# A hybrid decoder layer on one core: the head groups of the delta rule written out, their output moved to another buffer, and steps moved between pieces

## The chip, the cores and the metric

The kernel runs on one core of one Trainium2 chip. The metric is device time in microseconds (us), from the start of the program to its end. Three runs of the kernel before took 2874.61, 2876.35 and 2878.93 us; the median is 2876.35.

## What is computed

One layer of a decoder for a prompt of 256 tokens and 8 sample tokens (264 columns in all), with a model width of 2048. The part that matters here is the mixer's input projection and its branch A, the gated delta rule with 16 query/key heads and 32 value heads of width 128:

```python
proj = rmsnorm(h, attn_norm) @ w_in
q, k, v, z, a, b, sB, sC, sh, gA, gB = jnp.split(proj, IN_SPLITS, axis=-1)
qkv, new_qkv = causal_dwconv(jnp.concatenate([q, k, v], axis=-1), s_qkv, qkv_conv_w)
q, k, v = jnp.split(jax.nn.silu(qkv).astype(jnp.float32), (KEY_DIM, 2 * KEY_DIM), axis=-1)
q, k = l2norm(q), l2norm(k)                     # per head, each repeated for two value heads
...
decay = jnp.exp(jnp.where(lower, G[..., :, None] - G[..., None, :], -jnp.inf))
kk = jnp.einsum('bhncd,bhnsd->bhncs', k, k)
A = jnp.where(strict, beta[..., :, None] * kk * decay, 0.0)
sol = lax.linalg.triangular_solve(eye + A, rhs, left_side=True, lower=True)
...
o = rmsnorm(o, gdn_norm) * jax.nn.silu(z)       # gated output of each head
y_a = o.reshape(Bn, T, VAL_DIM) @ w_gdn_out
```

After the mixer come the merge with branch B, the output projection, a SwiGLU FFN, a per-layer input embedding and a final norm.

## The kernel before

Everything is written by hand per engine; the order within an engine is the order of the code, and the engines meet at semaphores. The weights stream from HBM in pieces of 4 row tiles x 256 columns (512 KB). For each piece SyncE starts the load into `raw` (4 buffers), ScalarE copies a rounded half `whi` (line 941, called here a split), VectorE subtracts to get the rest `wlo` (L1233), and TensorE does 24 matmuls over 264 columns (3 products for each of 8 blocks, L668). ScalarE and VectorE work three pieces ahead of TensorE. Four pieces make a pair of output tiles, which VectorE and ScalarE then scale, convolve and store (`evac`).

The columns of `w_in` for the delta rule are walked in 8 head groups, each of 4 value heads. A group is 32 pieces, numbered 0 to 31: k, q, v0, v1, z0, sc, sh and z1, four pieces each. The first group is a phase of its own ("first", with one more pair of four pieces ahead of it, so that its piece 0 is the phase's piece 4); the other seven are the phase "groups", a hardware loop of seven rounds; after it six pairs of sb columns ("last_group") carry the rest of the last group.

Between the pieces stand the steps of the delta rule. Three tables, `PE_STEP`, `ACT_STEP` and `DVE_STEP`, say after which piece of TensorE, and after which piece's split on ScalarE and VectorE, a step is placed; "cur" is the group whose columns are being made, "prev" the one before, whose last steps run during pieces 0 to 6 of the next. The steps spoken of here are:

- `exponents` (VectorE, L1285): differences of the cumulated decays, from `blk` into `E`; `exps` (ScalarE, L979, L980): their exponentials, into `EG` and `E`.
- `kk` (TensorE, L697 and the four matmuls behind it): transposes and products of the keys; it needs the SiLU of k (ScalarE, L1081, whose code stands after the split of piece 5), `exponents`, and `olog` of the group before, which frees its PSUM banks. `kcopy` (ScalarE, L984, L987) and `lt` (VectorE, L1314) make the lower triangle `Tt` from it.
- `blk_store` (ScalarE, L991): four DMAs write the 32x32 diagonal blocks of `Tt` to `blk_scratch`. GpSimd reads them back into `blk` (`blocks_in`, L556), solves them (`solve`, L535 to L542), writes `sol_scratch` (L564) and reads it into `DT` (L568). `blk` also holds the decay rows for `exponents`; they are loaded for the next group behind the solve (L548).
- `pt` (TensorE, after piece 25): the first products with `DT`. It waits for `DT` to land. `t1` stands after piece 31.
- `o1` (TensorE, after piece 3 of the next group), `osq`, `osum`, `oroot` and `o`: the output of the group, its norm, and its product with the gate in `o_all` (VectorE, L1361, L1366). The output stands in `E`, so that `exponents` of the next group waits for `o`.
- `qsum` after piece 11, with ones times the squares of q; `qn` on VectorE after the split at piece 13; `qk` on TensorE after piece 14.

GpSimd's queue of a group is, in order: two state loads of the group (`st_qkv`, L516, each waiting until TensorE has turned the state two loads before), `st_sc`, `finish` of the group before (stores, and a wait until they have landed), two state loads of the next group, `blocks_in`, `solve`, `solution_out`, the decay rows, `tails_out`. The first state load of the next group waits for TensorE's turn at piece 8, the second for the one at piece 12.

The functions that the diff touches, with the profile's line numbers:

Of the kernel before, what the change touches and what calls it, by code (L numbers as in the profile page):

```python
# [44 lines left out]
SB = 32  # L45
# [45 lines left out]
def trunk(nc, I, O):  # L91
# [133 lines left out]
    with ctx:  # L225
# [22 lines left out]
        ea_ready, diag_ready, tok_turned = (sem(n) for n in ("ea_ready", "diag_ready", "tok_turned"))  # L248
# [66 lines left out]
        nxt, cur = (lambda it: it + 1), (lambda it: it)  # L315
        const = lambda n: (lambda it: n)
        def layer_pairs(gx):
# [4 lines left out]
            Phase("groups", NG - 1, layer_pairs(nxt)),  # L322
# [54 lines left out]
        def cur_of(ph, it):  # L377

            return 0 if ph.name == "first" else it + 1 if ph.name == "groups" else None

        def prev_of(ph, it):

            return it if ph.name == "groups" else NG - 1 if ph.name == "last_group" else None

        def steps(table, ph, it, j):
# [3 lines left out]
            for which, gr in (("prev", prev_of(ph, it)), ("cur", cur_of(ph, it))):  # L389
                if gr is not None:  # L390
                    out += [(s, gr) for s in table[which].get(b, ())]
# [18 lines left out]
        PE_STEP = {"cur": {7: ("kk",), 11: ("qsum", "nturn"), 14: ("qk",), 18: ("tails",), 19: ("vturn",),  # L410
                           25: ("pt",), 26: ("pt0",), 27: ("pe0",), 28: ("pf0",), 29: ("s1",), 30: ("ks",), 31: ("t1",)},
                   "prev": {0: ("pt1",), 1: ("pe1",), 2: ("pf1",), 3: ("o1",), 4: ("osum",), 5: ("sct",)}}
        ACT_STEP = {"cur": {7: ("exps",), 8: ("kcopy",), 9: ("blk_store",), 10: ("qsq",), 12: ("qroot", "ncopy"),
                            19: ("stage",), 20: ("vcopy",), 25: ("t0c",), 27: ("f0c",), 29: ("s1c",), 31: ("t1c",)},
                    "prev": {1: ("f1c",), 3: ("osq",), 4: ("oroot",), 6: ("sct",)}}
        DVE_STEP = {"cur": {6: ("exponents",), 7: ("lt",), 13: ("qn",), 15: ("qkt",), 25: ("mask",), 26: ("e0",),
                            27: ("ktok",), 28: ("u0",), 30: ("r",)},
                    "prev": {0: ("e1",), 2: ("u1",), 3: ("s2",), 6: ("o",)}}
# [54 lines left out]
        def _(pool):  # L473
            mine = Count(pool_self)
            SOLVE_OPS = 2 * SB - 1
# [36 lines left out]
            def load_state(grp, i):  # L512
                if not (i < 2 and isinstance(grp, int) and grp == 0):
# [64 lines left out]
            def group(grp, first, last):  # L578
# [84 lines left out]
        def _(pe):  # L663
# [15 lines left out]
            def gdn(slot, gr):  # L679
# [990 lines left out]
```

## Time and profile before

| | |
|---|---|
| median of three runs | 2876.35 us |
| the profiled execution | 2873.98 us, its span 2872.4 us |
| TensorE matmul busy | 2694.1 us, 94% of the span |
| VectorE busy | 1658.9 us, 58% |
| ScalarE busy | 1344.4 us, 47% |
| GpSimd busy | 429.7 us, 15% |
| mean granted TensorE clock | 0.957 of full |
| HBM traffic | 175 GB/s over the span |

The rows below come from one profiled execution. PE is TensorE, DVE VectorE, ACT ScalarE, POOL GpSimd. A row of the timeline is start, duration, engine, line, operation, output<-inputs, tile sizes and count; in square brackets is the idle time of the engine before it and what ended that. A PE row's duration is that of pipelined matmuls, so the distance between starts tells more than the duration. The clock is given as a share of full speed (2.4 GHz); 0.5 is 1.2 GHz.

### The profile page before, as it was taken

The numbers are of one execution on the slowest core, as the hardware profiler recorded it, in microseconds if no ns is written. First come the engines' busy times: TensorE is split into PE (matmuls) and PEld (weight loads), VectorE is DVE, ScalarE is ACT, GpSimd is POOL, SyncE is SP. The second block draws the span as 40 slices with busy tenths as digits, with TensorE's granted clock in tenths as the row PEclk, the third lists the DMA queues.
The fourth block names the chain that finished last, engine by engine and source line by source line (L and its number), as shares of the span: only waits on it lengthen the run. The fifth ranks groups of instructions, "written<-read, shape, count | busy, mean of one in ns | idle before, by whom it ended". The sixth has DMA issues, their size and how long they took to land.

```text
span 2872.4 us, 57080 instructions
## 1 busy us (share of the span) xinstructions
PE 2694.1 (94%) x21133; PEld 2651.4 (92%) x21133; DVE 1658.9 (58%) x2851; ACT 1344.4 (47%) x2024; POOL 429.7 (15%) x813
## 2 busy tenths in 40 slices
PE   6989898888888989999999999899999999999997
PEld 4989898888888889999999999899999999999987
DVE  4747474747474656553335555555666656776664
ACT  4535353534344445443334434344555545665553
POOL 1324151515151505000000000000011000100000
PEclk9999999999999999999999999999999999999999
DMA  5545353535353535666665555755898566986552
GB/s 168 166 119 156 113 157 109 161 104 159 103 159 110 154 109 155 173 188 191 183 195 158 174 179 168 232 170 160 261 312 289 181 197 206 318 286 194 164 164 91
DMA packets 449338, 505.31 MB, mean 176 GB/s; under 512 B 27713, under 2 KB 429882, under 8 KB 446338
## 3 DMA queue, kind: packets, MB, share of 16 engines
q1 hardware_dynamic: 415264, 415.42, 48.1%
q0 software_dynamic: 24640, 86.42, 9.3%
q8 instruction: 120, 1.97, 0.3%
q10 hardware_dynamic: 9282, 1.24, 0.3%
q14 instruction: 32, 0.26, 0.0%
HBM read 477.10 MB, written 26.49 MB: 175 GB/s over the span
## 4 chain that ended last, share of the span: by engine, by line
PE 76%; POOL 8%; DMA 4%; issue 4%; DVE 3%; ACT 3%; POOLq 0%; ACTq 0%; DVEq 0%; SPq 0%
PE bank L668 75%; POOL prod L539 4%; POOL sol L542 4%; ACT whi L941 1%; DMA blk<-blk_scratch 1%; DMA raw<-in_w_ffn_down 1%; DMA raw<-in_w_o 1%; DMA sol_scratch<-sol 1%; DMA DT<-sol_scratch 1%; DVE wlo L1233 0%; ACT xhi L955 0%; DVE E L1285 0%; POOLq L73 0%; POOL sol_scratch L564 0%; POOL DT L568 0%
## 5 line engine op out<-in xcount | busy, mean ns | idle before, releaser
L668 PE MATMUL bank<-xhi,whi 128*128 128x264 f32 x5520 | 1618.9, 293 | 34.4 <-DVE wlo L1233 17.0
L668 PE MATMUL bank<-xlo,whi 128*128 128x264 f32 x5520 | 1593.3, 289 | 0.0
L668 PE MATMUL bank<-xhi,wlo 128*128 128x264 f32 x5520 | 1590.3, 288 | 0.0
L1233 DVE TENSOR_TENSOR wlo<-raw,whi 128x1024 fp32r<-128x1024 f32 x828 | 1012.1, 1230 | 817.6 <-ACT whi L941 815.4
L941 ACT ACTIVATE whi<-raw 128x1024 fp32r<-128x1024 f32 x828 | 872.3, 1058 | 926.3 <-PE bank L668 850.1
L668 PEld LDWEIGHTS bank<-xhi,whi 128*128 128x128 f32 x5520 | 1067.4, 193 | 40.9 <-issue 32.1
L668 PEld LDWEIGHTS bank<-xlo,whi 128*128 128x128 f32 x5520 | 1067.9, 193 | 2.6 <-issue 1.9
L668 PEld LDWEIGHTS bank<-xhi,wlo 128*128 128x128 f32 x5520 | 1064.4, 193 | 0.0
L668 PE MATMUL bank<-ahi,whi 128*128 128x264 f32 x704 | 200.6, 285 | 3.7 <-DVE wlo L1233 3.7
L668 PE MATMUL bank<-ahi,wlo 128*128 128x264 f32 x704 | 200.6, 285 | 0.0
L668 PE MATMUL bank<-alo,whi 128*128 128x264 f32 x704 | 200.2, 284 | 0.0
L668 PEld LDWEIGHTS bank<-ahi,whi 128*128 128x128 f32 x704 | 133.0, 189 | 3.9 <-DVE wlo L1233 3.9
L668 PEld LDWEIGHTS bank<-ahi,wlo 128*128 128x128 f32 x704 | 133.1, 189 | 0.0
L668 PEld LDWEIGHTS bank<-alo,whi 128*128 128x128 f32 x704 | 132.9, 189 | 0.0
L539 POOL TENSOR_TENSOR prod<-blk,sol 128x60 f32<-128x60 f32 (+24 forms) x248 | 117.3, 473 | 19.5
L542 POOL TENSOR_TENSOR sol<-sol,prod 128x60 f32<-128x60 f32 (+24 forms) x248 | 115.3, 465 | 19.4
L1378 DVE SCALAR_TENSOR_TENSOR cacc<-cin,vec,cacc 128x288 f32<-128x288 f32 x224 | 107.5, 521 | 14.8 <-DVE cacc L1376 2.3
L641 POOL DMA_DIRECT2D out_gdn_s<-sS x16 | 18.7, 1168 | 608.9 <-DVE sS L1597 608.9
L516 POOL DMA_DIRECT2D st_qkv<-in_state_qkv_conv x32 | 16.6, 520 | 532.0 <-PE bank L668 532.0
L1152 ACT ACTIVATE sS<-sS,bc 128x128 f32<-128x128 f32 x256 | 81.2, 392 | 0.0
L1597 DVE SCALAR_TENSOR_TENSOR sS<-sD,kqs,sS 128x128 f32<-128x128 f32 x256 | 72.6, 346 | 0.0
L668 PE MATMUL bank<-DT,Nn 128*128 128x128 f32 x128 | 28.0, 408 | 47.0 <-DMA DT<-sol_scratch 47.0
(279 smaller groups left out, 1902.5 us busy)
## 6 DMA issues: line engine op xcount, KB each, us to landing
raw<-in_w_in SPq DMA_DIRECT2D x356, 512.0 KB, 3.9
raw<-in_w_ffn_gate SPq DMA_DIRECT2D x88, 512.0 KB, 5.0
raw<-in_w_ffn_up SPq DMA_DIRECT2D x88, 512.0 KB, 4.7
raw<-in_w_ffn_down SPq DMA_DIRECT2D x96, 384.0 KB, 3.3
raw<-in_w_gdn_out SPq DMA_DIRECT2D x64, 512.0 KB, 3.6
chunkS<-in_state_gdn POOLq DMA_DIRECT2D x16, 1024.0 KB, 7.6
raw<-in_w_sconv_out SPq DMA_DIRECT2D x32, 512.0 KB, 3.6
raw<-in_w_o SPq DMA_DIRECT2D x32, 512.0 KB, 4.5
```

Of the source, the lines that this page charges most:

```text
L516: pool.dma_start(st_qkv[:, i % 2, :, :], stq[:, ds(STATE_COL[i](grp), COLS)].rearrange("r (t p) -> r t p", p=P)).then_inc(st_in[i % 2], 16)
L539: mine.inc(pool.tensor_tensor(prod[:, 0:m, 0:n], blk[:, j, j + 1:SB].unsqueeze(1).to_broadcast([P, m, n]), sol[:, 0:m, j:j + 1].to_broadca ...
L542: mine.inc(pool.tensor_tensor(sol[:, 0:m, j + 1:SB], sol[:, 0:m, j + 1:SB], prod[:, 0:m, 0:n], ALU.add))
L641: pool.dma_start(O["gdn_s"][0, 2 * b2 + s, 16 * c:16 * c + 16, :, :].rearrange("h k v -> k h v"), sS[:, s, :, :]).then_inc(n_stored[s], 16)
L668: return pe.matmul(out, lhsT, rhs, start=start, stop=stop)
L941: act.activation(whi[:, at_ % SPLIT, :, :], raw[:, at_ % RAW, :, :], ACT.Copy).then_inc(hi_ready, 1)
L1152: m = act.activation(sS[:, s, i, :], sS[:, s, i, :], ACT.Copy, scale=bc[:, ds(it * 2 + (s + 1), 1), 16 * c + i:16 * c + i + 1].rearrange(" ...
L1233: dve.tensor_tensor(wlo[:, at_ % SPLIT, :, :], raw[:, at_ % RAW, :, :], f32(whi[:, at_ % SPLIT, :, :]), ALU.subtract).then_inc(lo_ready, 1)
L1378: m = dve.scalar_tensor_tensor(out=cacc[:, t, :], in0=x, scalar=w, in1=cacc[:, t, :], op0=ALU.mult, op1=ALU.add)
L1597: m = dve.scalar_tensor_tensor(out=sS[:, s, i, :], in0=sD[:, s, i, :], scalar=kqs[:, 8 * c + i // 2, ds(it * 2 + s, 1), 0], in1=sS[:, s, i ...
```

## The change

The loop over seven groups becomes seven phases of straight code, on all engines; tests for "not the first group" that asked whether the group number was a register now ask for its value. The output of a group is copied into `vTok` instead of `E`, so `exponents` waits for `u1` of the group before instead of `o`, and `vcopy` (piece 20) waits for `o`. `exponents` moves from piece 6 to 3, `exps` from 7 to 4, `kk` and `lt` from 7 to 6, `kcopy` from 8 to 6, `nturn` from 11 to 10, `o` from 6 to 9. `kk` no longer waits for `exponents`. In the first group `exponents` and `exps` stand at 8 and 9 and `lt` at 9. The blocks are stored by GpSimd itself, and it loads the next group's first two states behind the solve instead of ahead of it.

```diff
-            Phase("groups", NG - 1, layer_pairs(nxt)),
+            *[Phase(f"group{n}", 1, layer_pairs(const(n))) for n in range(1, NG)],
...
-        PE_STEP = {"cur": {7: ("kk",), 11: ("qsum", "nturn"), 14: ("qk",), ...
+        PE_STEP = {"cur": {6: ("kk",), 10: ("nturn",), 11: ("qsum",), 14: ("qk",), ...
+                    "first": {9: ("exps",)}}
+                    "first": {8: ("exponents",), 9: ("lt",)}}
...
             def blocks_in(grp):
 
+                pool.wait_ge(g["lt"], grp + 1)
+                pool.sem_inc(pool_passed, 1)
+                for b in range(4):
+                    pool.dma_start(blk_d[:, b, :, :].rearrange("m j i -> j m i"),
+                                   Tt[SB * b:SB * b + SB, :, :].rearrange("p c (i t) -> p (c i) t", i=4)[:, :, SB * b:SB * b + SB]
+                                   ).then_inc(g["blk_stored"], 16)
                 pool.wait_ge(g["blk_stored"], grp * 64 + 64)
...
                 if not first:
                     finish(grp - 1)
-                if not last:
-                    load_state(grp + 1, 0)
-                    load_state(grp + 1, 1)
                 blocks_in(grp)
                 solve(grp)
                 solution_out(grp)
                 if not last:
                     decay_rows(grp + 1)
+                    load_state(grp + 1, 0)
+                    load_state(grp + 1, 1)
                 tails_out(grp)
...
-            with pool.Fori(0, NG - 2) as it_:
-                mine.enter(it_, SOLVE_OPS)
-                group(it_ + 1, False, False)
-            mine.leave(NG - 2)
+            for grp in range(1, NG - 1):
+                group(grp, False, False)
...
                 if slot == "kk":
                     pe.wait_ge(silu_done, 4 * gr + 1)
-                    pe.wait_ge(g["expo"], gr + 1)
-                    if not isinstance(gr, int):
+                    if gr > 0:
                         pe.wait_ge(g["olog"], gr)
+                    else:
+                        pe.wait_ge(tok_ready, 1)
...
-                elif slot == "blk_store":
-                    act.wait_ge(g["lt"], gr + 1)
-                    for b in range(4):
-                        act.dma_start(blk_d[:, b, :, :].rearrange("m j i -> j m i"), ...
...
                 elif slot == "vcopy":
                     act.wait_ge(g["vturned"], gr + 1)
                     act.wait_ge(g["klen"], gr + 1)
+                    act.wait_ge(g["o"], gr + 1)
...
-                    act.activation(E[:, 0, :], bank[6][:, :], ACT.Copy)
+                    act.activation(vTok[:, 0, :, :].rearrange("p b c -> p (b c)"), bank[6][:, :], ACT.Copy)
...
-                    act.activation(E[:, 1, :], bank[7][:, :], ACT.Copy)
+                    act.activation(vTok[:, 1, :, :].rearrange("p b c -> p (b c)"), bank[7][:, :], ACT.Copy)
...
                 if slot == "exponents":
                     dve.wait_ge(g["gb"], gr * 16 + 16)
-                    dve.wait_ge(g["o"], gr + 1)
+                    dve.wait_ge(g["u1"], gr) if gr > 0 else None
...
                 elif slot == "o":
                     dve.wait_ge(g["oroot"], gr + 1)
-                    mine.inc(dve.scalar_tensor_tensor(out=E[:, :, :], in0=E[:, :, :], scalar=vec[:, 368:369], ...
+                    ov = vTok[:, :, :, :].rearrange("p a b c -> p a (b c)")
+                    mine.inc(dve.scalar_tensor_tensor(out=ov, in0=ov, scalar=vec[:, 368:369], in1=PT[:, :, :], op0=ALU.mult, op1=ALU.mult))
                     mine.settle(dve)
                     for c in range(NCH):
                         o = o_all[:, ds(gr * 4, 4), c * CH:(c + 1) * CH]
-                        m = dve.tensor_tensor(o, o, H4(E, c), ALU.mult)
+                        m = dve.tensor_tensor(o, o, vTok[:, c, :, :], ALU.mult)
```

ScalarE, before, in a round of the loop, from the split at piece 6 to `kcopy` (`scb` is the staging of branch B's tail, `EG` and `E` are `exps`):

```order
L941 ACTIVATE whi<-raw 128x1024
L1036 REGISTER_ALU
L1038 ACTIVATE scb<-bank 10x256
L940 REGISTER_ALU
L941 ACTIVATE whi<-raw 128x1024
L979 ACT_TABLE_LOAD
L979 ACTIVATE EG<-blk 128x512
L980 ACTIVATE E<-E 128x1024
L940 REGISTER_ALU
L941 ACTIVATE whi<-raw 128x1024
L984 ACTIVATE Tt,ksum<-bank 128x128 x4
```

And in the changed kernel, a later group, from `oroot`'s exponential (`PT`) through the SiLU of k (`sqk`, `smp`) to `kcopy`:

```order
L1037 ACTIVATE PT<-PT 128x1024
L987 ACTIVATE EG<-blk 128x512
L988 ACTIVATE E<-E 128x1024
L949 ACTIVATE whi<-raw 128x1024
L1084 ACT_TABLE_LOAD
L1084 ACTIVATE sqk<-cacc 128x256
L1085 ACTIVATE smp<-cacc 128x8
L1084 ACTIVATE sqk<-cacc 128x256
L1085 ACTIVATE smp<-cacc 128x8
L949 ACTIVATE whi<-raw 128x1024
L1041 ACTIVATE scb<-bank 10x256
L992 ACTIVATE Tt,ksum<-bank 128x128 x4
```

`exps` now stands directly behind `oroot`, ahead of the SiLU of k; one table load and one split fewer stand between the SiLU and `kcopy`.

GpSimd, before, in a round of the loop, from the last store of `finish` to the solve (`sol<-unit` is its first operation):

```order
L526 DMA out_sc_s<-scb 8x256
L527 ISA
L528 ISA
L514 ISA
L516 ISA
L516 DMA st_qkv<-in_state_qkv_conv 24x256
L516 REGISTER_ALU
L516 DMA st_qkv<-in_state_qkv_conv 24x256
L553 ISA
L556 DMA blk<-blk_scratch 32x1024 x4
L535 COPY sol<-unit 128x256
```

And in the changed kernel:

```order
L530 DMA out_sc_s<-scb 8x256
L560 DMA blk_scratch<-Tt 32x8x32 x4
L566 DMA blk<-blk_scratch 32x1024 x4
L539 COPY sol<-unit 128x256
```

The two state loads, which waited for TensorE, have left this place; the four stores of the blocks have come to it.

VectorE in the changed kernel, a later group, from `s2` (`S`) through `exponents` to the end of the convolution of k (`cin`, `cacc`):

```order
L1359 SCALAR_TENSOR_TENSOR S<-S,bc,bank 128x128 x4
L1288 SCALAR_TENSOR_TENSOR E<-blk,tok,later 128x128 x8
L1442 TENSOR_TENSOR cin<-bank,rstd 128x256
L1443 TENSOR_TENSOR cin<-bank,rstd 128x8
L1444 TENSOR_TENSOR tail<-bank,rstd 128x11
L1445 COPY cin<-bank 128x8x3
L1442 TENSOR_TENSOR cin<-bank,rstd 128x256
L1443 TENSOR_TENSOR cin<-bank,rstd 128x8
L1444 TENSOR_TENSOR tail<-bank,rstd 128x11
L1445 COPY cin<-bank 128x8x3
L1379 TENSOR_SCALAR cacc<-cin,vec 128x288 x2
L1381 SCALAR_TENSOR_TENSOR cacc<-cin,vec,cacc 128x288 x6
```

Before, `exponents` stood behind `o`, behind the convolution and three splits. Now only the splits of pieces 7 to 9 stand between the convolution and `lt`, and `o` follows the convolution of q.

## Rows read from the trace of the kernel before

**Rows 1.** Waits of TensorE, 0 to 1150 us: total us, times, longest.
```profile
PE bank L668 <- DMA DT<-sol_scratch: 47.0, 7, 8.4
PE bank L697 <- DVE E L1285: 36.8, 8, 5.2
PE bank L668 <- issue: 18.3, 6, 3.2
```

**Rows 2.** Timeline of TensorE: `kk` of three groups, and piece 6 of one.
```profile
225.27 1.11 PE L697 MATMUL bank<-ident,sqk 128*128 128x128 f32 x4 [5.15 <-DVE E L1285]
...
497.12 0.37 PE L668 MATMUL bank<-xhi,whi 128*128 128x264 f32 x1
...
508.32 1.11 PE L697 MATMUL bank<-ident,sqk 128*128 128x128 f32 x4 [5.14 <-DVE E L1285]
...
1077.45 1.11 PE L697 MATMUL bank<-ident,sqk 128*128 128x128 f32 x4 [5.15 <-DVE E L1285]
```

**Rows 3.** Timeline of TensorE: marks in the first group and behind the last.
```profile
89.42 0.63 PE L697 MATMUL bank<-ident,sqk 128*128 128x128 f32 x4 [0.81 <-DVE E L1285]
...
101.88 0.36 PE L668 MATMUL bank<-xhi,whi 128*128 128x264 f32 x1 [1.47 <-DVE wlo L1233]
104.87 1.02 PE L668 MATMUL bank<-QK,ones 128*128 128x512 f32 x2
...
186.99 1.05 PE L668 MATMUL bank<-vTok,DT 128*128 128x128 f32 x8
187.97 0.62 PE L668 MATMUL bank<-ident,st_qkv 24*128 24x24 f32 x4
...
202.95 0.38 PE L668 MATMUL bank<-EG,S 128*128 128x128 f32 x2
...
1094.42 1.02 PE L668 MATMUL bank<-QK,ones 128*128 128x512 f32 x2
...
1141.24 1.95 PE L668 MATMUL bank<-DT,Nn 128*128 128x128 f32 x16
...
1166.77 1.05 PE L668 MATMUL bank<-vTok,DT 128*128 128x128 f32 x8
```

**Rows 4.** Timeline of ScalarE: `oroot`, the split behind k's SiLU, `exps`, the next split.
```profile
496.83 1.06 ACT L1034 ACTIVATE PT<-PT 128x1024 f32<-128x1024 f32 x1
...
501.00 1.04 ACT L941 ACTIVATE whi<-raw 128x1024 fp32r<-128x1024 f32 x1
...
508.30 0.63 ACT L979 ACTIVATE EG<-blk 128x512 f32<-128x512 f32 x1 [3.74 <-DVE E L1285]
...
509.79 1.04 ACT L941 ACTIVATE whi<-raw 128x1024 fp32r<-128x1024 f32 x1
```

**Rows 5.** Timeline of VectorE: `o` and `exponents` of one group.
```profile
503.22 1.28 DVE L1361 SCALAR_TENSOR_TENSOR E<-E,vec,PT 128x1024 f32<-128x1024 f32 x1
...
506.08 2.19 DVE L1285 SCALAR_TENSOR_TENSOR E<-blk,tok,later 128x128 f32<-128x128 f32 x8
```

**Rows 6.** Stretches behind two short waits: length, busy (count) per engine, granted clock, DMA.
```profile
1631.90:1636.00 4.10, 4.05 (x33) 4.05 (x34) 4.10 (x13) 2.49 (x5) 0.00 (x0) 1.00 0.03 8
1851.70:1856.00 4.30, 4.25 (x22) 4.25 (x23) 0.00 (x0) 0.00 (x0) 0.00 (x0) 0.60 1.03 376
```

**Rows 7.** Timeline of GpSimd: last state load ahead of `blocks_in`; the last group's blocks.
```profile
528.15 0.51 POOL L516 DMA_DIRECT2D st_qkv<-in_state_qkv_conv  x1 [15.17 <-PE bank L668]
...
1089.53 1.97 POOL L556 DMA_DIRECT2D blk<-blk_scratch  x4 [16.46 <-DMA blk_scratch<-Tt]
1094.41 0.40 POOL L535 COPY sol<-unit 128x256 f32<-128x256 f32 x1 [2.91 <-DMA blk<-blk_scratch]
...
1134.92 2.32 POOL L568 DMA_DIRECT2D DT<-sol_scratch  x4 [3.18 <-DMA sol_scratch<-sol]
```

**Rows 8.** DMA issues by line: count, KB of each, median us to landing.
```profile
blk_scratch<-Tt ACTq DMA_DIRECT2D x32, 32.0 KB, 1.7
sol_scratch<-sol POOLq DMA_DIRECT2D x32, 32.0 KB, 2.6
```

More of the change, by code:

```diff
@@ L247, in trunk @@
             sem(n) for n in ("soft_in", "soft_ready", "g_ready", "rows_ready"))
-        ea_ready, diag_ready, tok_turned = (sem(n) for n in ("ea_ready", "diag_ready", "tok_turned"))
+        ea_ready, diag_ready, tok_turned, tok_ready = (sem(n) for n in ("ea_ready", "diag_ready", "tok_turned", "tok_ready"))
         z_scaled = sem("z_scaled")
@@ L313, in spair @@
             return mk(win, lambda it: b + gx(it) * COLS, X, kind, gx, xr="attn")
-        nxt, cur = (lambda it: it + 1), (lambda it: it)
+        cur = (lambda it: it)
         const = lambda n: (lambda it: n)
@@ L377, in cur_of @@
         def cur_of(ph, it):
-            return 0 if ph.name == "first" else it + 1 if ph.name == "groups" else None
+            return 0 if ph.name == "first" else int(ph.name[5:]) if ph.name.startswith("group") else None
         def prev_of(ph, it):
-            return it if ph.name == "groups" else NG - 1 if ph.name == "last_group" else None
+            return int(ph.name[5:]) - 1 if ph.name.startswith("group") else NG - 1 if ph.name == "last_group" else None
         def steps(table, ph, it, j):
@@ L390, in steps @@
                 if gr is not None:
-                    out += [(s, gr) for s in table[which].get(b, ())]
+                    at_b = table[which].get(b, ())
+                    if ph.name == "first" and "first" in table:
+                        at_b = table["first"].get(b, tuple(s for s in at_b if not any(s in v for v in table["first"].values())))
+                    out += [(s, gr) for s in at_b]
             return out
@@ L407, in freed_all @@
                 eng.wait_ge(pair_free[m % 2], m // 2 + 1)
-        PE_STEP = {"cur": {7: ("kk",), 11: ("qsum", "nturn"), 14: ("qk",), 18: ("tails",), 19: ("vturn",),
+        PE_STEP = {"cur": {6: ("kk",), 10: ("nturn",), 11: ("qsum",), 14: ("qk",), 18: ("tails",), 19: ("vturn",),
                            25: ("pt",), 26: ("pt0",), 27: ("pe0",), 28: ("pf0",), 29: ("s1",), 30: ("ks",), 31: ("t1",)},
                    "prev": {0: ("pt1",), 1: ("pe1",), 2: ("pf1",), 3: ("o1",), 4: ("osum",), 5: ("sct",)}}
-        ACT_STEP = {"cur": {7: ("exps",), 8: ("kcopy",), 9: ("blk_store",), 10: ("qsq",), 12: ("qroot", "ncopy"),
+        ACT_STEP = {"cur": {4: ("exps",), 6: ("kcopy",), 10: ("qsq",), 11: ("ncopy",), 12: ("qroot",),
                             19: ("stage",), 20: ("vcopy",), 25: ("t0c",), 27: ("f0c",), 29: ("s1c",), 31: ("t1c",)},
-                    "prev": {1: ("f1c",), 3: ("osq",), 4: ("oroot",), 6: ("sct",)}}
-        DVE_STEP = {"cur": {6: ("exponents",), 7: ("lt",), 13: ("qn",), 15: ("qkt",), 25: ("mask",), 26: ("e0",),
+                    "prev": {1: ("f1c",), 3: ("osq",), 4: ("oroot",), 6: ("sct",)},
+                    "first": {9: ("exps",)}}
+        DVE_STEP = {"cur": {3: ("exponents",), 6: ("lt",), 13: ("qn",), 15: ("qkt",), 25: ("mask",), 26: ("e0",),
                             27: ("ktok",), 28: ("u0",), 30: ("r",)},
-                    "prev": {0: ("e1",), 2: ("u1",), 3: ("s2",), 6: ("o",)}}
+                    "prev": {0: ("e1",), 2: ("u1",), 3: ("s2",), 9: ("o",)},
+                    "first": {8: ("exponents",), 9: ("lt",)}}
         NORM = {"first": 0, "ffn0r": 1, "pgate_first": 2}
@@ L512, in load_state @@
             def load_state(grp, i):
-                if not (i < 2 and isinstance(grp, int) and grp == 0):
+                if i >= 2 or grp > 0:
                     pool.wait_ge(st_turned, grp * 4 + (i - 1))
@@ L703, in gdn @@
                     pe.wait_ge(g["qsq"], gr + 1)
-                    if not isinstance(gr, int):
+                    if gr > 0:
                         pe.wait_ge(g["s2"], gr)
@@ L708, in gdn @@
                     pe.wait_ge(g["qn"], gr + 1)
-                    if not isinstance(gr, int):
+                    if gr > 0:
                         pe.wait_ge(sct_staged, gr)
@@ L999, in gdn @@
                     act.wait_ge(tails_turned, gr + 1)
-                    if not isinstance(gr, int):
+                    if gr > 0:
                         act.wait_ge(tails_stored, 96 * gr)
@@ L1226, in _ @@
             dve.sem_inc(g["o"], 1)
-            dve_per = {"groups": 20, "gates": 0, "yb1": 0, "ya0": 2, "ya1": 2, "wo": 0,
+            dve_per = {"gates": 0, "yb1": 0, "ya0": 2, "ya1": 2, "wo": 0,
                        "ffn0s": 2, "ffn1s": 2, "down0": 0, "down1": 0, "pgate": 2}
@@ L1551, in extra @@
                     mine.settle(dve)
+                    dve.sem_inc(tok_ready, 1)
                 elif ph.name in NORM and j == 3:
```

6 lines of the change are left out of this document (removed).

## The prediction

> **What bounds the kernel now.** I read the page's busy shares first: TensorE has work in 94% of the span, so a gain can only come from its idle time or its clock. The waits of TensorE up to 1150 us, the stretch of the head groups, come next. Three kinds recur once a group: for `DT`, 47.0 us in 7 waits; for `exponents` ahead of `kk`, 36.8 us in 8, nearly all of it in seven of about 5.15; and 18.3 us in 6 put down to "issue" [rows 1]. These six stand at the turns of the loop, ahead of the first state turn of a round. The loop is seven rounds, so it turns six times.
>
> Next I took the length of a group from `kk` to `kk`. From the second group (225.27) to the last (1077.45) it is 852.18 / 6 = 142.03 us [rows 2]. What TensorE would need without a wait at full clock I put together from stretches where it had none [rows 3]: `kk` to `qsum` 104.87 - 89.42 - 1.47 = 13.98; `qsum` to `pt` 1141.24 - 1094.42 = 46.82; `pt` to `t1` 1166.77 - 1141.24 = 25.53; `t1` to the turn of the next group 187.97 - 186.99 = 0.98; turn to `o1` 202.95 - 187.97 = 14.98; `o1` to the point where `kk` could begin 225.27 - 5.15 - 202.95 = 17.17 [rows 2, 3]. The sum is 119.5. So 22.5 us of each group are not work. The waits are (47.0 - 8.4) / 6 = 6.4 (the first group's 8.4 left out) + 5.15 + 18.3 / 6 = 3.05, together 14.6 [rows 1, 2]. The other 7.9 us I put down to matmuls at half clock behind the three waits.
>
> **The turn of the loop.** Straight code leaves no branch. Between the first group and the loop, where the code is straight too, TensorE went from `t1` to the turn in 0.98 us without a wait [rows 3]. I take the 3.05 us and the slow clock behind them as gone. If only the branch goes and something else waits there, nothing is gained; that is a rival below. Register instructions in the other engines' queues go as well; I cost them at nothing, since these engines are ahead of TensorE except where named below.
>
> **`exponents` and `kk`.** In one group pieces 6 and 7 take 508.32 - 5.14 - 497.12 = 6.06, so 3.0 us each, and piece 6 ended at about 500.15 [rows 2]. `kk` now stands there. `exponents` (2.19 us) moves ahead of the convolution of k on VectorE and is no longer waited for [rows 5]; the convolution gets 2.2 us later and stays ahead of ScalarE. What is late next is the SiLU of k. Before, it was done when the next split began, at 501.00 [rows 4]. Now `exps` stands ahead of it, directly behind `oroot`: 509.79 - 508.30 = 1.49 us, without a table load of its own, because `oroot` ends in the same function [rows 4]. So k is ready at 501.00 + 1.49 = 502.5, and `kk` waits 2.3 us with a handover. Bounds: 0.8 if `exps` costs this path nothing, 4.5 if the late convolution costs it another 2.2. I take 2.3. The piece that leaves the stretch before `kk` comes behind it: no gain and no loss.
>
> **The blocks.** Before, GpSimd reached `blocks_in` only after the state load that waits for TensorE's turn at piece 12 (a wait of 15.17), at 528.15 [rows 7]. In the last group, which has no such loads, it waited for the blocks alone, and TensorE took up `pt` with no wait [rows 3, 7]. That group is the model for all. There, from `kk`: blocks landed after 1089.53 - 1077.45 = 12.1; solve begun after 17.0; the four loads of `DT` issued from 57.5 to 59.8, landed, with the 2.6 of a like GpSimd transfer, at about 62.4 [rows 2, 7, 8]. GpSimd stores the blocks itself now. Four transfers of this size take it as long to issue as the loads of `DT`, 2.3 us, where ScalarE needs a little less, and land in 2.6 instead of 1.7 [rows 7, 8]: up to 1.4 later. But `kk` at full clock ends 1.3 sooner. TensorE reaches `pt` at 13.98 + 3.0 (piece 7) + 46.82 = 63.8 us after `kk`. So `DT` lands 1 to 3 us ahead, and the 6.4 us go with their slow clock. The cover is thin: a solve longer by 3 us uses it up.
>
> **`o` at piece 9.** It took 506.08 - 503.22 = 2.86 us of VectorE [rows 5]. It leaves the path ahead of `kk` and goes between `lt` and `qn`, while `lt` no longer has the split of piece 10 ahead of it. TensorE is nearer to VectorE there than before. I add 1.3 us of wait for `qn`; bounds 0 and 2.9, the whole of `o`.
>
> **Clock.** Behind a wait of 2.56 us the granted clock was 1.00, behind one of 1.91 us 0.60 [rows 6]; so the rows leave open whether 2.3 us costs speed. The three stops of a group cost 7.9 / 3 = 2.6 each. Where the clock falls the wait for `qn` shrinks, since TensorE arrives later. I take 0.8 us a group for both together, bounds 0 and 2.6. The Trainium skill, TensorE: Matmul & The Clock Gate, section Part 1, says that the throttled clock is the default state and that activity releases it; the two rows show that a short wait can go either way. Were each wait to cost the full step, the group would be 1.8 us longer than I take it.
>
> **The sum.** A group: 119.5 + 2.3 + 1.3 + 0.8 = 123.9, against 142.0: 18.1 less, times six, 109. The first group hardly gains: its `lt` moves behind the convolution of q and gets later by about the 7 us that `blocks_in` no longer waits, so `DT` lands near where it did, and its 8.4 us wait stays [rows 1]; bounds minus 5 and plus 5. Its successor's `kk` gains 5.15 - 2.3 = 2.9, and its move by one piece is 3.0, which comes back behind the last `kk`. The last group has no `DT` wait to lose; behind its `kk` it gains about 1.8 of clock and pays 1.3 at `qn`. That makes 109 + 3 = 112. The profiled execution took 2873.98, so it would take 2762. The median before was 2876.35, 2.4 more; I forecast 2763 for the median.
>
> **Rivals.**
> 1. `DT` stays last. For it: the cover is 1 to 3 us, and the solve now lies beside the convolutions of v0 and v1 and `qkt`. Against it: it took no wait in the last group. If it lands 2 us late and the clock falls behind it, a group costs 2.0 + 2.6 = 4.6 more: 7 x 4.6 = 32, hence 2795. Chance 0.17.
> 2. The turn's cost stays, because it was no branch but something else that happens at a group's start. The six "issue" waits speak for it, the smooth start of the second group against it. 6 x (3.05 + 2.6) = 34, hence 2797. Chance 0.07.
> 3. The written-out code itself stops the engines: seven groups of instructions that are fetched once each, where a loop had one. Place: the instruction supply of TensorE; price: that of a turn, 3.05 + 2.6 = 5.65 us a stop. It decides from 112 / 5.65 = 20 stops, three a group. With four a group, 28 x 5.65 = 158, the kernel takes 2763 + 158 = 2921. Against it: up to 1150 us, with the whole first group in straight code, the six turns are the only "issue" waits of TensorE [rows 1]. Chance 0.05. The Trainium skill, Runtime: NRT & Kernel Launch, section Instruction fetch mechanics, says that the sequencer fetches ahead in order and hides it, and that a taken branch breaks this; by that the stops vanish and this rival with them.
>
> **Numbers.** My forecast has 0.71. Its own range is 2745 (no clock loss, no wait at `qn`: 6 x 2.1 less, and the first group plus 5) to 2787 (`kk` waiting 4.5 and the clock falling behind it, 4.0 a group more). The range reaches to rivals 1 and 2: 2740 to 2800. A measurement of this kernel can tell 0.2%, about 6 us, from no change. Faster: 0.71 + 0.17 + 0.07 = 0.95, less 0.01 for mishaps that eat exactly the gain; same 0.01; slower 0.05.
>
> **What the profile after would show.** Right: no "issue" wait of TensorE in the groups; `kk` waiting about 2.3 us for the SiLU of k on ScalarE, not for VectorE's `E`; waits for `DT` gone but for the first group's 8 us; `kk` to `kk` near 124 us; GpSimd's wait for TensorE ahead of the blocks gone. Wrong: a `DT` wait in each group (rival 1), waits at the first state turn (rival 2), "issue" waits strewn over pieces (rival 3), or a wait of TensorE for `wlo` or `sqk` from VectorE above 3 us a group, which would mean that I underrated VectorE's queue between `lt` and `qn`.

## The result and the profile after

The kernel after takes 2788.78 us (median of four runs, 2780.30 to 2792.23); the kernel before took 2875.54 beside it. The ratio is 0.9692, with a 95% interval of 0.9669 to 0.9715: 3.1% faster. The profiled execution took 2788.91 us, its span 2787.2, with a mean clock of 0.971 of full (0.957 before). The forecast was 2763. The time lies in the stated range (2740 to 2800), but only because that range reached out to rivals 1 and 2; the forecast's own ended at 2787. The likeliest case was not the one that happened: the waits for `DT` stayed, which was rival 1 (2795, chance 0.17).

TensorE's waits in the head groups, the view of [rows 1], total, times and longest:

```profile
PE bank L675 <- DMA DT<-sol_scratch: 30.0, 8, 5.6
PE bank L705 <- ACT smp L1085: 16.4, 7, 2.3
PE bank L675 <- DVE wlo L1236: 9.9, 2, 6.3
PE bank L728 <- DVE Tt L1317: 4.2, 1, 4.2
```

The "issue" waits are gone. `kk` waits for the SiLU of k (L1085), 2.35 us in each of seven groups, where it waited 5.15 for VectorE before. The third row is not new: before, the wait for `wlo` was 12.6 us in 4, the longest 6.3 as here. But `DT` is still waited for in all eight groups; four of the waits, and `kk` of the second, the sixth and the last group, from the timeline (start, duration, line, operation, idle time before):

```profile
160.16 3.75 PE L675 MATMUL bank<-DT,Nn 128*128 128x128 f32 x16 [4.87 <-DMA DT<-sol_scratch]
221.23 1.12 PE L705 MATMUL bank<-ident,sqk 128*128 128x128 f32 x4 [2.35 <-ACT smp L1085]
415.01 2.02 PE L675 MATMUL bank<-DT,Nn 128*128 128x128 f32 x16 [0.74 <-DMA DT<-sol_scratch]
730.92 0.66 PE L705 MATMUL bank<-ident,sqk 128*128 128x128 f32 x4 [2.35 <-ACT smp L1085]
797.95 3.56 PE L675 MATMUL bank<-DT,Nn 128*128 128x128 f32 x16 [3.58 <-DMA DT<-sol_scratch]
926.64 3.75 PE L675 MATMUL bank<-DT,Nn 128*128 128x128 f32 x16 [5.57 <-DMA DT<-sol_scratch]
986.83 0.66 PE L705 MATMUL bank<-ident,sqk 128*128 128x128 f32 x4 [2.35 <-ACT smp L1085]
```

A group is (986.83 - 221.23) / 6 = 127.6 us, against 142.0 before and 123.9 forecast. Over groups 2 to 7 the wait for `DT` is 3.6 us on average (0.74 to 5.57). GpSimd's part of the group whose `kk` is at 730.92, to be set beside [rows 7]:

```profile
737.73 2.39 POOL L560 DMA_DIRECT2D blk_scratch<-Tt  x4 [4.03 <-issue]
743.09 2.00 POOL L566 DMA_DIRECT2D blk<-blk_scratch  x4 [2.97 <-DMA blk_scratch<-Tt]
750.00 0.40 POOL L539 COPY sol<-unit 128x256 f32<-128x256 f32 x1 [4.92 <-DMA blk<-blk_scratch]
785.83 2.35 POOL L574 DMA_DIRECT2D sol_scratch<-sol  x4 [0.74 <-POOLq L548]
792.04 2.32 POOL L578 DMA_DIRECT2D DT<-sol_scratch  x4 [3.87 <-DMA sol_scratch<-sol]
```

The solve (750.00 to 785.83, 35.8 us) is nearly as long as before (over the seven later groups 36.1 us on average, from `sol<-unit` to the store of the solution, against 35.4). The transfers are not: GpSimd waits 4.92 us for the blocks where it waited 2.91 in the last group before [rows 7], and 3.87 for the solution. The solve begins 19.1 us after `kk`, not 17.0. The windows of this stretch (us; busy time and count of PE, PEld, DVE, ACT, POOL; clock; DMA share; GB/s) and SyncE's weight loads, issued 6.9, 12.9 and 17.7 us after `kk`:

```profile
742.92:744.92 2.00, 2.00 (x20) 2.00 (x19) 2.00 (x3) 2.00 (x6) 1.83 (x4) 1.00 0.26 68
744.92:746.92 2.00, 2.00 (x20) 2.00 (x19) 1.97 (x3) 2.00 (x4) 0.17 (x1) 1.00 0.85 224
746.92:748.92 2.00, 2.00 (x16) 1.77 (x15) 2.00 (x3) 0.13 (x2) 0.00 (x0) 1.00 1.09 290
748.92:750.92 2.00, 2.00 (x13) 1.44 (x12) 1.96 (x10) 1.98 (x2) 0.76 (x3) 1.00 1.08 300
```

```profile
737.78 0.37 SPq L447 DMA_DIRECT2D raw<-in_w_in  x1
743.79 1.50 SPq L447 DMA_DIRECT2D raw<-in_w_in  x2
748.58 1.50 SPq L447 DMA_DIRECT2D raw<-in_w_in  x2
```

The DMA engines are full (share 0.85 to 1.09) from two us after the first block load is issued until the blocks have landed: the 4 x 128 KB of the blocks run beside two or more weight loads of 512 KB. The weight loads go out when VectorE's `wlo` frees a buffer, and after the convolution of q VectorE does two or more `wlo` in a row, so they come in bunches. Here the two `wlo` ahead of the loads at 743.79 and 744.92, and, of the last group before, the four weight loads that started 1.6 us after its block load [rows 7]:

```profile
742.54 2.35 DVE L1236 TENSOR_TENSOR wlo<-raw,whi 128x1024 fp32r<-128x1024 f32 x2
```

```profile
1091.14 3.88 SPq L442 DMA_DIRECT2D raw<-in_w_in  x4
```

After the change the first of the bunch starts 0.7 us after the block load.

### The profile page after: what moved, and what is told of

Same layout as the page of the kernel before. It is cut to its first block, busy times and chain, and to the rows that moved or that the text cites. A ratio compares the mean times of both kernels' runs of the same rounds, so it can differ in the third digit from the quotient of the medians.

```text
span 2787.2 us, 54613 instructions
## 1 busy us (share of the span) xinstructions
PE 2666.2 (96%) x21133; PEld 2624.0 (94%) x21133; DVE 1656.3 (59%) x2851; ACT 1327.5 (48%) x2010; POOL 452.5 (16%) x845
## 4 chain that ended last, share of the span: by engine, by line
PE 58%; DMA 2%; POOL 1%; ACT 1%; DVE 1%; issue 1%; DVEq 0%; ACTq 0%; SPq 0%; POOLq 0%
PE bank L675 58%; DMA raw<-in_w_o 1%; POOL sol L546 1%; POOL prod L543 1%; ACT xhi L963 0%; DMA raw<-in_w_ffn_down 0%; ACT whi L949 0%; DVE wlo L1236 0%; DVE h L1644 0%; DMA blk<-blk_scratch 0%; DMA raw<-in_w_ple_gate 0%; PE bank L924 0%; DVE xlo L1264 0%; DMA DT<-sol_scratch 0%; DMA sol_scratch<-sol 0%
## 5 line engine op out<-in xcount | busy, mean ns | idle before, releaser
L675 PE MATMUL bank<-xhi,whi 128*128 128x264 f32 x5520 | 1610.7, 292 | 32.6 <-DVE wlo L1236 14.5
L546 POOL TENSOR_TENSOR sol<-sol,prod 128x60 f32<-128x60 f32 (+24 forms) x248 | 127.6, 514 | 19.5
L543 POOL TENSOR_TENSOR prod<-blk,sol 128x60 f32<-128x60 f32 (+24 forms) x248 | 109.6, 442 | 19.5
L622 POOL DMA_DIRECT2D chunkS<-in_state_gdn x16 | 18.5, 1157 | 286.7 <-PE bank L675 153.3
```

Source lines behind the costliest of these rows:

```text
L543: mine.inc(pool.tensor_tensor(prod[:, 0:m, 0:n], blk[:, j, j + 1:SB].unsqueeze(1).to_broadcast([P, m, n]), sol[:, 0:m, j:j + 1].to_broadca ...
L546: mine.inc(pool.tensor_tensor(sol[:, 0:m, j + 1:SB], sol[:, 0:m, j + 1:SB], prod[:, 0:m, 0:n], ALU.add))
L622: pool.dma_start(chunkS[:, c, :, :], I["state_gdn"][0, b, 16 * c:16 * c + 16, :, :].rearrange("h k v -> k h v")).then_inc(s_in[c], 16)
L675: return pe.matmul(out, lhsT, rhs, start=start, stop=stop)
```

## The experiments

Each was timed against the kernel before on the same chip, which took 2874.6 to 2874.9 us there. The kernel after was not timed again beside them, so differences from it are between medians, and its own runs lie 12 us apart: a few us tell nothing. The question behind most of them is whether the chain from `kk` through blocks, solve and `DT` ends last and weight traffic lengthened its transfers; each expectation says what its theories A and B are. Waits and lengths of groups come from one traced execution of each.

**The loop put back.** Everything else as after.

```diff
-            *[Phase(f"group{n}", 1, layer_pairs(const(n))) for n in range(1, NG)],
+            Phase("groups", NG - 1, layer_pairs(nxt)),
```

> The changed kernel with the loop of seven rounds put back; the buffers, the tables and GpSimd's order stay as changed. Theory A (the turn of the loop costs TensorE a wait of about 3.05 us and some 2.5 us of half clock behind it, and straight code removes both): six waits put down to issue come back, the group goes from 127.6 to about 133, the kernel from 2789 to about 2822. Rival B (something else that happens at a group's start made those waits, and they went because k's states are now loaded early): no such waits, 2789 within 6.

Measured 2803.38 us, ratio 0.9753 (0.9729 to 0.9776): 14.6 above the kernel after, between the two. Its waits:

```profile
PE bank L678 <- DMA DT<-sol_scratch: 19.5, 8, 4.7
PE bank L678 <- issue: 18.2, 6, 3.2
```

The turn is back at its full price: 3.0 us idle, and from `ks` to `o1` 24.6 us on average instead of 19.8, so 4.8 a turn with the clock, 29 in six. But the wait for `DT` fell from 30.0 to 19.5 in total. So about half of what the unrolling takes away at the turn is lost again, by the longer waits for `DT`.

**The unrolling alone**, on the kernel before (the same edit the other way round):

> The kernel before with nothing but its loop over the groups written out. Theory A (the turn costs its idle time and the slow clock behind it, and nothing takes its place): 6 x (3.05 + 2.6) = 34 us less than before, about 2841 us; no wait for issue, waits for DT still near 6.4 us a group. Rival B (part of the turn was cover: while TensorE stood at it, the weight loads stood still too, and without it the small transfers land later and DT with them): the kernel after gained only 14.6 us from the same edit, so 2875 - 15 = 2860 us, with the waits for DT 1 to 2 us longer each.

Measured 2837.60 us, ratio 0.9873 (0.9853 to 0.9894): 37 us less than the kernel before. Theory A held. The waits for `DT` stayed (48.0 in 7, [rows 1] had 47.0), and `ks` to `o1` fell from 25.3 to 19.8 us, 5.6 a turn, 33 in six. The view still has a row of "issue":

```profile
PE bank L694 <- issue: 35.3, 7, 5.0
```

These are the seven waits of `kk` (L694), which [rows 1] puts down to `E`; at the places of the turns there is none. So the turn is worth 33 to 37 us where `DT` takes no part of it back.

**The next group's states loaded ahead of the blocks again:**

```diff
                     finish(grp - 1)
+                if not last:
+                    load_state(grp + 1, 0)
+                    load_state(grp + 1, 1)
                 blocks_in(grp)
```

> The changed kernel with the two state loads of the next group put back ahead of the blocks in GpSimd's queue. Theory A (this queue position alone held the solve back): GpSimd reaches the store of the blocks only at TensorE's turn at piece 12, about 12 us later than now, DT lands as much later, the wait of TensorE for it goes from 3.6 to about 15 us a group, the kernel to about 2870 or more, near the kernel before. Rival B (the blocks were ready late anyway, and the order hardly mattered): DT wait within 3 us of now, the kernel below 2815.

Measured 2848.90 us, ratio 0.9906 (0.9881 to 0.9932): 60 above the kernel after. Theory A in kind; it had asked for 20 more.

```profile
PE bank L676 <- DMA DT<-sol_scratch: 93.3, 8, 14.2
```

```profile
517.98 0.58 POOL L520 DMA_DIRECT2D st_qkv<-in_state_qkv_conv  x1 [12.52 <-PE bank L676]
518.56 2.36 POOL L560 DMA_DIRECT2D blk_scratch<-Tt  x4
531.72 0.40 POOL L539 COPY sol<-unit 128x256 f32<-128x256 f32 x1 [6.46 <-DMA blk<-blk_scratch]
```

The block store stands 20.3 us after `kk` (498.25) instead of 6.8. Without the new order of GpSimd's queue the earlier `kk` buys nothing: the kernel before with the unrolling alone takes 2837.60.

**Three quarters of the weight bytes left out** in the seven later groups: one of four row tiles is loaded, and all the products are still made.

```diff
+                        r = 1 if ph.name.startswith("group") else n
-                        sp.dma_start(raw[:, p % RAW, 0:n, :], q.rows[:, kt:kt + n, ...
+                        sp.dma_start(raw[:, p % RAW, 0:r, :], q.rows[:, kt:kt + r, ...
```

> The changed kernel, but in the seven later groups SyncE loads only one of the four row tiles of each weight piece (a quarter of the bytes; the other three keep what an earlier piece left). All else is the same. Theory A (the transfers of the chain from lt to DT land late because they fall beside bursts of weight loads: blk lands after 4.8 to 6.1 us instead of 2.9, sol_scratch after 3.8 instead of 2.5, DT after 3.6 instead of 2.1): they land as in the kernel before, the DT waits of the later groups (0.7 to 5.6, mean 3.6) shrink below 1 us, the group falls from 127.6 to 122 to 124, the kernel to about 2760. Rival B (they land late because GpSimd now issues all of them and its own queue is slow): the landings stay above 4.5 and the DT waits stay near 3.6; the kernel within 8 us of 2789.

Measured 2753.07 us, ratio 0.9574 (0.9552 to 0.9595). Theory A. The only wait for `DT` left is that of the first group, where the weights are whole:

```profile
PE bank L706 <- ACT smp L1086: 16.4, 7, 2.3
PE bank L676 <- DMA DT<-sol_scratch: 4.8, 1, 4.8
```

```profile
591.87 2.48 POOL L561 DMA_DIRECT2D blk_scratch<-Tt  x4 [3.66 <-DVE Tt L1318]
596.25 1.99 POOL L567 DMA_DIRECT2D blk<-blk_scratch  x4 [1.89 <-DMA blk_scratch<-Tt]
600.79 0.82 POOL L540 COPY sol<-unit 128x256 f32<-128x256 f32 x1 [2.55 <-DMA blk<-blk_scratch]
```

With `kk` at 585.45 the solve begins after 15.3 us; after the change it is 20.0 on average. A group is 122.9 us in each of six. The engines' instructions are the same, so 4.7 us a group are the traffic's: 3.6 of wait and 1.6 of slow clock behind it, less some 0.8, since behind the wait of `kk` the clock fell here in all seven groups (`kk` to `qsum` 19.1 us).

**The first group's triangle two pieces earlier** (`exponents` 6, `exps` and `lt` 7).

> The changed kernel with exponents, exps and lt of the first group at pieces 6, 7 and 7 instead of 8, 9 and 9. Theory A (the late lt of the first group made TensorE's wait of 4.2 us for it at nturn and keeps DT at 160 us): both waits (4.2 and 4.9) and their slow clock go, the kernel gets 9 to 14 us faster, about 2777. Rival B (the first group's DT is late for the landings, not for lt): only the 4.2 goes and DT still waits 4 us or more, 2 to 6 us faster.

Measured 2786.66 us (2774.78 to 2792.76), ratio 0.9676 (0.9645 to 0.9706), 2 below the kernel after, which is no difference by this noise. By the waits it is nearly rival B: in the first group the 4.2 at `nturn` is gone and `DT` is still waited for, 3.5 us. That group did gain (the next `kk` at 212.62 instead of 221.23), but in the traced execution, the slowest of the four (2792.76), the later groups took (990.28 - 212.62) / 6 = 129.6 us, with the waits for `DT` at 4.4 on average. No step in them was changed. Runs of this kernel lie 18 us apart, those of the kernel after 12. That the place of their transfers against the weight loads differs from run to run would explain both; it is not shown.

**The block store back on ScalarE:**

```diff
-        ACT_STEP = {"cur": {4: ("exps",), 6: ("kcopy",), 10: ("qsq",), ...
+        ACT_STEP = {"cur": {4: ("exps",), 6: ("kcopy",), 8: ("blk_store",), 10: ("qsq",), ...
```

> The kernel after, with the store of the blocks back in ScalarE's queue (at piece 8, in the first group at 10). Theory A (the weight traffic slows every small transfer, whichever queue it is in): the store lands 2.7 to 3.3 us after its issue as it does from GpSimd, and the time is within 4 us of the kernel after, 2785 to 2791 us. Rival B (it is GpSimd's queue that made it slow): the store lands in 1.7 us as in the kernel before, the blocks and DT come 1.3 us sooner in all eight groups, 2789 - 8 x 1.3 = 2779 us or, with the clock, less.

Measured 2772.93 us (2767.00 to 2790.03), ratio 0.9663 (0.9627 to 0.9700). The median is nearer to rival B; the interval holds both. In the trace, which is of the fastest of its four executions, the median store lands in 1.7 us, as before the change, while from GpSimd it took 3.3; the wait for the blocks, whose load is still GpSimd's but starts a little earlier, is 4.7 us instead of 5.5, and the wait for `DT` 2.2 instead of 3.6. A group is (969.62 - 219.28) / 6 = 125.1 us. So this part of the change cost up to 2.5 us a group; I had bounded it at 1.4 and taken it as covered.

**`kk` back behind piece 7** (`exponents` 4, `exps` 5, `kcopy` and `lt` 7, `nturn` and `ncopy` one piece later too; in the first group 6, 7, 7 and 7).

```diff
-        PE_STEP = {"cur": {6: ("kk",), 10: ("nturn",), 11: ("qsum",), ...
+        PE_STEP = {"cur": {7: ("kk",), 11: ("qsum", "nturn"), ...
```

> The kernel after, with the keys' product back behind piece 7 (exponents at 4, exponentials at 5, copies and triangle at 7). Theory A (DT ends last, so that the products that start the chain set the group): the wait of kk goes from 2.35 us to none, but kk starts 3.0 - 2.35 = 0.65 us later against the pieces, and the wait for DT grows from 3.6 to about 6.6 us; 7 x 0.65 = 5 us more, about 2794 us. Rival B (DT lands in time by itself and the early product is only a wait of its own): 7 x 2.35 = 16 us less, 2773 us.

Measured 2758.11 us (2756.01 to 2761.64), ratio 0.9589 (0.9570 to 0.9609): 31 below the kernel after. Theory A's number was wrong by 36 us, rival B's reason too, since `DT` is still waited for (16.9 in 7):

```profile
339.06 2.46 POOL L560 DMA_DIRECT2D blk_scratch<-Tt  x4 [4.09 <-DVE Tt L1317]
343.42 1.99 POOL L566 DMA_DIRECT2D blk<-blk_scratch  x4 [1.89 <-DMA blk_scratch<-Tt]
350.67 0.41 POOL L539 COPY sol<-unit 128x256 f32<-128x256 f32 x1 [5.26 <-DMA blk<-blk_scratch]
```

```profile
344.35 1.50 SPq L447 DMA_DIRECT2D raw<-in_w_in  x2
```

With `kk` at 332.62, the store goes at 6.4 us after it and lands in 1.89, with no weight load issued beside it: the first bunch goes out at 11.7. In the kernel after one went at 6.9, with the store. The block load at 10.8 runs into the bunch and takes 5.26. So `kk` comes later in pieces, but the chain is 2.0 us shorter (in the groups that wait for it, TensorE takes `DT` up 65.8 us after `kk` instead of 67.8), and the 2.35 of waiting for the SiLU are gone. A group is 124.8 us. The first group gives the rest: its next `kk`, one piece further on, is at 210.05 instead of 221.23.

**The same with light weights:**

> kk behind piece 7 as in the run before, with a quarter of the weight bytes in the seven later groups (three of four row tiles are not loaded; the products are made from what is left in the buffer). With kk behind piece 6 the same lightening gave 2753 us and no wait for DT but the first. Theory A (with fast landings the early product buys nothing and costs its wait of 2.35 us a group, and the first group is 13 us shorter with kk at 7): a group of about 121.8 us instead of 122.9, and 2753 - 7 - 13 = 2733 us. Rival B (what kk at 7 gained is a lucky place of the bursts alone): about 2753 us.

The same three quarters of the weight bytes are left out. Measured 2729.36 us, ratio 0.9498 (0.9477 to 0.9519). Theory A: a group is (940.96 - 209.73) / 6 = 121.9 us. Against the lightened kernel with `kk` at 6 this is 24 us less. The two traced executions differ by 15.5: 7 up to the `kk` of the second group, which stands one piece further on here, 1.0 in each of the six groups, and 2 behind them; where the other 8 of the medians lie no trace shows. So with fast transfers `kk` at 6 brings no gain. The gain of `kk` at 7 is smaller than the wait of 2.35 that it removes, since that kernel has short waits for `EG` (5.2 us in 8) and two for `DT` in the later groups, one of 3.05 us:

```profile
PE bank L676 <- DMA DT<-sol_scratch: 4.1, 3, 3.0
```

**All steps from `pt` to `osum` one piece later**, `kk` at 6.

```diff
-  25: ("pt",), 26: ("pt0",), 27: ("pe0",), 28: ("pf0",), 29: ("s1",), 30: ("ks",), 31: ("t1",)},
-  "prev": {0: ("pt1",), 1: ("pe1",), 2: ("pf1",), 3: ("o1",), 4: ("osum",), 5: ("sct",)}}
+  26: ("pt",), 27: ("pt0",), 28: ("pe0",), 29: ("pf0",), 30: ("s1",), 31: ("ks",)},
+  "prev": {0: ("t1",), 1: ("pt1",), 2: ("pe1",), 3: ("pf1",), 4: ("o1",), 5: ("osum", "sct")}}
```

> The kernel after, with all steps from pt to osum one piece later (pt behind piece 26, t1 behind piece 0 of the next group, o1 behind 4, osum behind 5). Theory A (what is missing is 1 to 5 us between the landing of DT and pt): the wait for DT falls from 3.6 us to about 0.6 a group and its slow clock goes; kk waits about 1.2 us more, since oroot now stands right ahead of the SiLU of k on ScalarE; 8 x (3.0 + 1.5 - 1.2) = 26 us less, 2763 us. Rival B (the room only moves the wait: kk waits 5 us and more behind osum and oroot, with a slow clock of its own): 2785 us or more.

Measured 2776.64 us, ratio 0.9653 (0.9633 to 0.9673), halfway:

```profile
PE bank L705 <- ACT smp L1085: 31.1, 7, 4.5
PE bank L675 <- DMA DT<-sol_scratch: 8.3, 4, 4.8
```

The wait for `DT` fell from 30.0 to 8.3 us, and that for the SiLU rose from 16.4 to 31.1: 4.45 each, where I had allowed 3.55. A wait was moved, and the clock fell behind it (`kk` to `qsum` 19.2 to 20.3 us, where it is 17.6 without a fall).

**`o` at piece 16**, on the kernel with `kk` at 7.

> The kernel with kk behind piece 7 of the run before, and o moved on from piece 9 to piece 16 of VectorE. In that run TensorE waited 10.2 us in 8 waits for EG (ahead of qk) and 7.9 us more for wlo than the kernel after. Theory A (DT still lands last, so those waits only hide a longer one behind them): TensorE reaches pt sooner, waits for DT as much longer, and the time stays at 2758, within 6 us. Rival B (VectorE's queue is a cost of its own): 18 us less, about 2740 us.

Measured 2773.69 us (2771.41 to 2779.01), ratio 0.9662 (0.9648 to 0.9676): 16 slower than with `o` at 9. Both theories fell. VectorE's `wlo`, SyncE's loads and GpSimd's wait in the group with `kk` at 461.85:

```profile
472.32 4.73 DVE L1236 TENSOR_TENSOR wlo<-raw,whi 128x1024 fp32r<-128x1024 f32 x4
473.57 3.88 SPq L447 DMA_DIRECT2D raw<-in_w_in  x4
481.48 0.61 POOL L539 COPY sol<-unit 128x256 f32<-128x256 f32 x1 [6.85 <-DMA blk<-blk_scratch]
```

Where `o` had stood between the second and the third `wlo`, VectorE now does four `wlo` in a row (4.73 us), and four weight loads go out within 3.9 us, on top of the block load. GpSimd waits 6.85 us for the blocks here and 5.7 on average over seven groups, against 5.3 with `o` at 9, and TensorE's wait for `EG` rises from 10.2 to 14.3. The profiled executions of the two differ by 10 us, 8 of them in the six groups. That the bunching makes the difference is my reading of these rows; no run changes the bunching alone.

**The store on ScalarE and `sol<-unit` ahead of the wait**, added to that:

> The same with the block store in ScalarE's queue behind piece 9, and GpSimd's copy of unit into sol made before its wait for the blocks. Theory A (DT lands last; each us taken from the chain from kk to DT is a us of the group): the copy is 0.75 us, the issue and the landing of the store some 0.7, together 1.5 x 8 = 12 us less than the kernel before it in this list. Rival B (the landings follow the bursts of weights and eat what is saved): no less than it.

Measured 2744.88 us (2741.43 to 2751.21), ratio 0.9560 (0.9545 to 0.9574): 29 less, not 12. In the group with `kk` at 451.76:

```profile
461.25 1.98 POOL L560 DMA_DIRECT2D blk<-blk_scratch  x4 [7.14 <-DMA blk_scratch<-Tt]
463.23 0.48 POOL L537 COPY sol<-unit 128x256 f32<-128x256 f32 x1
466.26 0.89 POOL L543 TENSOR_TENSOR prod<-blk,sol 128x31 f32<-128x31 f32 x1 [2.55 <-DMA blk<-blk_scratch]
```

```profile
463.48 3.97 SPq L447 DMA_DIRECT2D raw<-in_w_in  x4
```

The block load is issued 9.5 us after `kk`, 1.3 earlier, ahead of the same bunch at 11.7. It is in after 14.5 us; in the run before, after 19.6. A load that starts 1.3 us earlier lands 5 earlier; over the seven later groups it starts 1.0 earlier and the last of the blocks lands 3.7 earlier (14.7 us after `kk` instead of 18.4). This run changes two things at once, and what each gave is not shown. And ScalarE's split waits less for weights (15.2 us in 7 waits instead of 23.4 in 6 from 210 to 960 us), TensorE's wait for `EG` falls from 14.3 to 1.6.

**The steps from `pt` to `osum` one piece later, on top:**

> The same again, with all steps from pt to osum one piece later, exponents at 3 and exps at 4. Theory A (3 us more room for DT, and with kk at 7 the late oroot leaves its SiLU in time): no wait for DT but in the first group, kk waiting at most 1 us, a group of 120.5 us where kk at 7 alone had (958.83 - 210.05) / 6 = 124.8; 7 x 4.3 = 30 us less than 2758, about 2728 us. Rival B (kk waits 2 us or more behind oroot, exps and the SiLU, and the clock falls): 2745 us or more.

Measured 2743.30 us (2739.41 to 2746.77), ratio 0.9551 (0.9537 to 0.9564), within 2 us of the run before it and nearer to rival B. The wait for `DT` is down to 2.7 us in 2, and `kk` waits 1.5 in each group. These last two are the fastest kernels here with the whole computation: 4.4 to 4.5% less than before, where the change alone took 3.1%.

## Why the prediction was right and where it was not

*The turn.* Right: no "issue" wait is left. It is worth what was reckoned, 34, when taken alone (37 measured), and 15 at the end of this change, since the thin `DT` took part of it back. The Trainium skill, Runtime: NRT & Kernel Launch, section Instruction fetch mechanics, says that straight code is fetched ahead and a taken branch breaks that; the traces agree, with no such stop of TensorE in seven groups of straight code and 3.0 us at each turn, in both pairs of kernels that differ by the loop alone. That it is the fetch, and not another part of the loop, no run here separates. Rivals 2 and 3 fell with it.

*`kk`.* Right to 0.05 us: 2.35 us for the SiLU of k, 2.3 forecast. `kk` to the next pieces and `o1` to `kk` (14.24, forecast 17.17 - 3.0) came as worked out.

*`qn`.* Forecast 1.3, measured 0.3 us in one group and none in the others. Why is open: with the loop kept, and `kk` to `qsum` the same 17.6 us, TensorE waits there for `EG` 0.8 to 1.0 us in six groups.

*The blocks: the step that failed.* The step was: "So `DT` lands 1 to 3 us ahead, and the 6.4 us go with their slow clock." It landed 3.6 us behind on average, though the order of queues was as said. I took the landing times of block and solution transfers from the last group before [rows 7] and the medians [rows 8]. In that group the block load went out 1.6 us ahead of a bunch of weight loads, as shown above. Landed blocks at 12.1 and a solve at 17.0 after `kk` were copied into a group whose `kk`, and with it the transfers, stands elsewhere against those loads. Measured over seven groups, GpSimd waited 3.1 us for the store where I took 2.6, 5.5 for the blocks instead of 2.9, and 3.6 for the solution instead of the 3.2 of the last group. The solve took 36.1 where that group had 35.0. Together `DT` was in 67.8 us after `kk` and not 62.4, and TensorE came for it after 64.2, near the 63.8 of the forecast. With the weights lightened the transfers are as fast as I took them: no wait for `DT` in the later groups, a group of 122.9 (forecast 123.9) and 2753 us in all. "The cover is thin: a solve longer by 3 us uses it up" named the right place but looked at the solve alone, which gave 1.1 of the 5.4. Rival 1 had the price: 4.6 us a group for a late `DT` and its clock, where 3.6 and 1.6 were measured.

Not all of it is traffic. In the fourth and the seventh group GpSimd stood still by itself around the store of the solution, 1.97 us between two of its four parts, and 2.92 us ahead of it instead of 0.74:

```profile
533.49 0.56 POOL L574 DMA_DIRECT2D sol_scratch<-sol  x1 [1.97 <-issue]
917.61 2.33 POOL L574 DMA_DIRECT2D sol_scratch<-sol  x4 [2.92 <-issue]
```

Of the later groups these have the two longest waits for `DT`, 4.70 and 5.57. All nine kernels here in which GpSimd stores the blocks have both stops, in the same two groups, also with the loop kept and with the weights lightened; one of them is behind the wait of 3.05 in the lightened kernel with `kk` at 7. The kernel before and the four others, where ScalarE stores the blocks, have a single one, of about 2.3 us, between the loads of `DT` of one group. So part of what the store on ScalarE gave may be one stop less. What causes the stops no run shows.

*The clock.* Forecast 0.8 us a group. Behind the wait of 2.35 us the clock fell in three of the seven groups (`kk` to `qsum` 19.1 us instead of 17.6) and not in four, so 1.5 x 3 / 7 = 0.6 there. The rest is behind the `DT` waits, 1.6 us a group: at 289.77 it was 0.56 for 3.2 us, while the wait of 0.74 at 415.01 left it at 1.00:

```profile
289.77:293.00 3.23, 3.23 (x17) 3.23 (x18) 0.00 (x0) 0.00 (x0) 1.50 (x4) 0.56 0.47 171
415.00:419.00 4.00, 3.99 (x35) 4.00 (x36) 1.29 (x2) 1.04 (x2) 1.04 (x3) 1.00 0.63 193
```

The Trainium skill, TensorE: Matmul & The Clock Gate, Part 1, has throttled as the default that activity lifts. The rows agree: work brings the clock back, to 1.00 from 293 us on. But a stop of 2.35 us decides nothing by itself, with a fall behind it in three groups and none in four.

*The first group.* Forecast: `DT` "lands near where it did, and its 8.4 us wait stays". It was 4.2 for `nturn` (waiting for `Tt`, which I did not name) and 4.87 for `DT`, together 9.1, much the same. That it need not be so is shown by the run with `kk` at 7 and that group's tables earlier: 1.0.

*The sum.* A group took 3.7 us more than forecast, 22 in six, and first and last together 4.5 more: 27, the whole difference between 2762 and 2789. The excess of a group is the 3.6 of wait and the 1.6 of clock behind it, less the 1.3 at `qn` that did not come. The change gave 87 us: the order of GpSimd's queue holds 60 (lost when it is undone), and the unrolling 15; parts priced in this way need not add up to the whole. `kk` at 6 was a loss of its own: undone, together with earlier tables in the first group, it gave 31, of which 17 in the six later groups.

## What to carry to other kernels

A landing time read in one stretch holds for the traffic of that stretch. When a step moves, ask what other queue issues within 5 us of its transfers at the new place, and read which engine's work frees that queue's buffers. When a chain through DMAs ends last with a few us to spare, try its start against the bunches of bulk loads in both directions: a later start may land sooner. And price each part by undoing it from the whole, not only by adding it to the start; the unrolling was 37 us one way and 15 the other.

## What was not expected of the hardware

Four loads of 128 KB took 2.55 us of waiting after their issue beside lightened weight loads, and 6.85 beside four loads of 512 KB, with a DMA share of 1.0 to 1.1 over the last 6 us. Issued 1.3 us earlier, ahead of the bunch, they were in 3.0 us after the last issue. The same small store took 1.7 us from ScalarE's queue and 3.3 from GpSimd's in medians over the whole kernel with `kk` at 6, but 1.9 from GpSimd's and 1.9 to 2.0 from ScalarE's with `kk` at 7: here the time of its issue counted more than the queue.
